# Attention in half units: order of scores, maxima, exponentials and copies in a kernel of three transformer-like blocks

## The chip, the cores and the metric

One core of a Trainium2 chip runs the whole program. The metric is the time on the device in microseconds (us) of one execution; the kernel before is told by the median of three runs and one profiled execution. Engines: PE is TensorE (PEld its weight loads), DVE VectorE, ACT ScalarE, POOL GpSimd, SP SyncE, which issues the weights' transfers. Each runs its own instructions in order; they wait for one another by semaphores.

## The reference

A hybrid layer (a gated linear recurrence, sparse attention, gated linear attention, merged, and a feed-forward part) is followed by two blocks (each: half a feed-forward part, a mixer, half a feed-forward part) on 256 tokens and 256 context tokens of width 1024, all in fp32. Cut to what matters here, three attentions, 64 wide heads:

```python
# hybrid layer, 16 heads in 4 groups: compressed, selected and windowed keys, each its own softmax
p = softmax(q @ k.T + bias)            # over 15 compressed, 256 selected, 256 windowed keys
o = g[0] * o_cmp + g[1] * o_slc + g[2] * o_win
# even block: 8 heads in 2 groups, window of 128 and 256 context keys, a sink logit per head
p = softmax(concatenate([s_loc, s_ctx, s_sink]))
# odd block: 8 heads, neighbourhood of the grid with a bias, and 256 context keys
p = softmax(concatenate([s_loc + bias, s_ctx]))
o = p @ v
```

## The kernel before

Weights pass through a ring of three slots in SBUF; TensorE multiplies them in split form (lines 817 to 819: high and low parts), which is most of the program. Between such stages stand three attentions. Each is a loop over units: a unit is (kind, g, t), 4 heads of group g for the 128 queries of tile t. UNITS lists 8 of kind nsa (units 0 to 7, t alternates 0, 1), 8 of kind ev (8 to 15, t = 0 to 3 for each of two g; for t = 2 and 3 the queries are context tokens and only the 256 context keys are scored), 4 of kind od (16 to 19). An nsa unit with t = 0 scores 128 keys per head and kind of key (small), one with t = 1 256 (large).

PSUM holds one unit's scores in banks 0 to 3 (nsa: and the compressed ones in bank 4), two turned batches in banks 5 and 6, and the output in bank 7. A unit goes through the engines so:

- TensorE, scores(u): per head r the product of queries and keys into PSUM; nsa at line 1059 (compressed keys 1046), ev and od at 1079. A head's bank must be free: free(b) waits for part b of the exponentials of unit u - 1 (for nsa r = 0 waits for part 1 and r = 1 for part 3). Two signals, att_score, go out, one when heads 0 and 1 (nsa: 0 and 2) are there, one at the end.
- VectorE, att_max(u): in two halves, each waits for its att_score: bias or mask added in PSUM (2226, 2244), negated maximum (2227, 2246), in ev two small steps for the sink (2251, 2253); signal att_max each.
- ScalarE, att_exp(u, part), four parts: exponentials from PSUM to one of two SBUF buffers, with row sums (1588, compressed 1593; 1600, and 1598 for the sink). Parts 0 and 2 wait for a half of the maxima.
- VectorE, att_norm(u): after all four parts. For nsa it multiplies the exponentials with gate over sum (2263 to 2279); for ev and od it makes four diagonal matrices from the reciprocals (2282, 2283, 2285). Signal att_p.
- TensorE, att_out(u): waits for att_p, then per batch of 128 keys turns the four heads' exponentials (a transpose at 1105, for ev and od a product with the diagonal matrices at 1110), and, one batch behind, multiplies the turned batch with the values (1135; od 1125).
- ScalarE, att_copy(u, i): a turned batch from PSUM to SBUF (1611).
- VectorE, att_done(u): the unit's output from PSUM (2295).

A unit has 3 (nsa, t = 0), 5 (nsa, t = 1), 4 or 2 (ev, t >= 2) batches. The order on each engine is written out by hand. TensorE: scores(u + 1), att_out(u). VectorE: att_norm(u), both halves of att_max(u + 1), att_done(u). ScalarE: copy 0, copy 1, part 0 of u + 1, copy 2, part 1, copy 3, part 2, copy 4, part 3 (copies that a unit doesn't have left out):

```python
for i in range(5):
    if i < len(batches(u)):
        att_copy(u, PT, i)
    if i >= 1 and u + 1 < u1:
        att_exp(u + 1, Pb, i - 1)
```

Of the kernel before, what the change touches and what calls it, by code (L numbers as in the profile page):

```python
# [335 lines left out]
def build(nc, d, out_x):  # L336
# [5 lines left out]
    with ctx:  # L342
# [73 lines left out]
        CMP_AT = 4 * BANK  # L416

# [339 lines left out]
        def _(pe):  # L757
# [273 lines left out]
            def scores(u):  # L1031
# [7 lines left out]
                if kind == "nsa":  # L1039
# [10 lines left out]
                    for r in range(4):  # L1050
                        half = slice(64 * (r % 2), 64 * (r % 2) + 64)
                        if r < 2:
                            free(1 + 2 * r)
                        if r == 2:
                            compressed(0).then_inc(sig("cmp_even"), 1)
                        for seg in range(2):
                            kk = (B_kk if g % 2 == r % 2 else B_ks)[half, 2 * seg + g // 2, 0:nk]
                            at = place(seg, r) * S
                            last = mm(psum[:, at:at + nk], B_q[half, 2 * g + r // 2, t * P:(t + 1) * P], kk,
                                      start=True, stop=True)  # L1060
                        if r == 2:
                            last.then_inc(sig("att_score"), 1)
# [226 lines left out]
        def _(act):  # L1289
# [284 lines left out]
            def att_exp(u, Pb, part):  # L1574
# [3 lines left out]
                nm, sm = small[:, 0:12], small[:, 16:28]  # L1578
# [16 lines left out]
                else:  # L1595
                    k0 = S if t >= 2 else 0
                    if kind == "ev" and part % 2 == 0:
                        A(small[:, 32 + part:34 + part], small[:, 28 + part:30 + part], ACT.Exp)
# [15 lines left out]
            def attention(u0, u1, Pb, PT):  # L1614
# [3 lines left out]
                for u in range(u0, u1):  # L1618
                    for i in range(5):
                        if i < len(batches(u)):  # L1620
                            att_copy(u, PT, i)
                        if i >= 1 and u + 1 < u1:
                            att_exp(u + 1, Pb, i - 1)
# [92 lines left out]
        def _(dve):  # L1716
# [495 lines left out]
            def att_max(u):  # L2212
# [3 lines left out]
                for a in range(2):  # L2216
# [30 lines left out]
                    if kind == "ev":  # L2247
# [5 lines left out]
                        ins = v.tensor_tensor(out=small[:, 28 + 2 * a:30 + 2 * a], in0=sink, in1=nma, op=ALU.add)  # L2253
                    ins.then_inc(sig("att_max"), 1)

            def att_norm(u, Pb):
                kind, g, t = UNITS[u]
                sm = small[:, 16:28]
# [22 lines left out]
                if kind == "ev":  # L2281
                    link(v.tensor_tensor(out=sm[:, 0:4], in0=sm[:, 0:4], in1=small[:, 32:36], op=ALU.add))
                link(v.reciprocal(small[:, 36:40], sm[:, 0:4]))

# [14 lines left out]
            def attention(u0, u1, Pb, y):  # L2299
                att_max(u0)  # L2300
                for u in range(u0, u1):
                    att_norm(u, Pb)
                    if u + 1 < u1:
                        att_max(u + 1)
# [267 lines left out]
```

## Time and profile before

| | |
|---|---|
| median of 3 runs | 2484.18 us (2484.06 to 2491.02) |
| profiled execution | 2482.93 us, its span 2481.0 us |
| PE busy | 2354.6 us (95% of the span) |
| DVE / ACT / POOL busy | 1565.3 / 873.7 / 378.1 us |
| mean granted clock of TensorE | 0.969 of full speed |
| chain that ended last | PE 83%, DVE 10%, ACT 3% |

The page has the engines' busy times, the span in 40 slices with the granted clock of TensorE (1.0 is 2.4 GHz, 0.5 is 1.2 GHz), the chain of waits that ended last, and the costliest groups of instructions by line of the kernel. A TensorE that is busy for 95% of the span leaves some 126 us without work, a good part of them in the attentions. In the views by order of time a row is a merged run of like instructions: start, duration until the end of the last one, engine, line, what is written and read, shapes, count, and in brackets the idle time before it and what ended it. The ends of matmuls are modelled and overlap the next row's start, so starts are compared with starts.

### The profile page before, as it was taken

Reading aid. Unit: us, or ns where it says so; the run is one execution under the profiler, and the core shown is the slowest. Engines: PE = TensorE matmul, PEld = TensorE weight load, DVE = VectorE, ACT = ScalarE, POOL = GpSimd, SP = SyncE. Lnnn points to the kernel's source line nnn. Section 1 sums busy time; section 2 is a strip of 40 time slices with the busy share of each in tenths; the row PEclk is TensorE's granted clock in tenths of the full one; section 3 lists DMA queues with packets and bytes.
Section 4 is the critical chain, followed back from the end, with each engine's and each line's share of the span. In section 5 each row is a group of like instructions: output and inputs, shape, how many; then the busy total and the mean of one; then the engine's idle time right before and its main releaser. Section 6 shows DMA issues by size and latency. Waiting matters only on the chain.

```text
span 2481.0 us, 33593 instructions
## 1 busy us (share of the span) xinstructions
PE 2354.6 (95%) x14384; PEld 2034.6 (82%) x14384; DVE 1565.3 (63%) x1954; ACT 873.7 (35%) x1241; POOL 378.1 (15%) x345
## 2 busy tenths in 40 slices
PE   7999988797999999999989999999999999888999
PEld 7998875597998888888857888888888888777999
DVE  6584545557876887876764977634855434685554
ACT  6744324534444212123443422212422212444332
POOL 0020000121220313120010221201221201101111
PEclk9999987898999999999999999999999999999999
DMA  5453451063653544542300445322445322511453
GB/s 220 170 187 137 141 191 67 1 224 150 252 198 128 200 173 174 199 153 102 107 35 35 167 175 201 136 94 94 165 177 201 136 94 94 153 69 69 170 200 107
DMA packets 34689, 356.29 MB, mean 144 GB/s; under 512 B 3965, under 2 KB 6172, under 8 KB 8428
## 3 DMA queue, kind: packets, MB, share of 16 engines
q1 hardware_dynamic: 31644, 343.67, 37.4%
q0 software_dynamic: 2896, 10.46, 1.6%
q8 instruction: 114, 1.87, 0.3%
q14 instruction: 35, 0.29, 0.0%
HBM read 351.15 MB, written 1.13 MB: 142 GB/s over the span
## 4 chain that ended last, share of the span: by engine, by line
PE 83%; DVE 10%; ACT 3%; issue 2%; DMA 1%; POOL 1%; SPq 0%; DVEq 0%; ACTq 0%
PE psum L817 25%; PE psum L818 24%; PE psum L819 24%; PE psum L1110 2%; DVE ring_r L1740 2%; DVE arena L2340 1%; DMA ring<-in_w 1%; DVE rr L1750 1%; PE psum L1161 1%; ACT arena L1588 1%; PE psum L1105 1%; PE psum L1079 1%; PE psum L1135 1%; PE psum L1015 1%; ACT arena_r L1325 1%
## 5 line engine op out<-in xcount | busy, mean ns | idle before, releaser
L817 PE MATMUL psum<-arena_r 128*128 128x256 f32 (+1 forms) x3368 | 1131.0, 336 | 33.0 <-DVE zT_r L1780 14.4
L819 PE MATMUL psum<-arena_r,ring_r 128*128 128x256 f32 (+1 forms) x3368 | 1121.4, 333 | 0.0
L818 PE MATMUL psum<-zT_r,arena_r 128*128 128x256 f32 (+1 forms) x2640 | 862.2, 327 | 0.0
L1325 ACT ACTIVATE arena_r<-ring 128x2048 fp32r<-128x2048 f32 (+1 forms) x252 | 473.6, 1881 | 844.1 <-PE psum L819 800.9
L1740 DVE TENSOR_TENSOR ring_r<-ring,arena_r 128x2048 fp32r<-128x2048 f32 (+1 forms) x252 | 595.2, 2363 | 214.3 <-ACT arena_r L1325 213.1
L817 PEld LDWEIGHTS psum<-arena_r 128*128 128x128 f32 x3368 | 638.0, 189 | 110.5 <-issue 16.5
L819 PEld LDWEIGHTS psum<-arena_r,ring_r 128*128 128x128 f32 x3368 | 639.7, 190 | 69.2
L818 PEld LDWEIGHTS psum<-zT_r,arena_r 128*128 128x128 f32 x2640 | 503.5, 191 | 46.0
L818 PE MATMUL psum<-arena_r 128*128 128x256 f32 (+1 forms) x1304 | 424.2, 325 | 0.0
L1892 DVE CUSTOM_DVE_ANT_0 psum<-arena,cb 128x1024 f32<-128x1024 f32 x256 | 363.7, 1479 | 0.0
L818 PEld LDWEIGHTS psum<-arena_r 128*128 128x128 f32 x1304 | 246.6, 189 | 20.3
L711 POOL CAST arena_r<-rt 128x512 fp32r<-128x512 f32 (+1 forms) x55 | 57.2, 1039 | 910.4 <-DVE rt L1953 910.4
L1827 DVE SCALAR_TENSOR_TENSOR xT<-psum,gates_h,xT 128x256 f32<-128x256 f32 x168 | 75.3, 479 | 133.7 <-PE psum L819 133.2
L817 PE MATMUL psum<-xT_r,arena_r 128*128 128x256 f32 x512 | 145.4, 284 | 9.0 <-DVE zT_r L1778 8.3
L819 PE MATMUL psum<-xT_r,ring_r 128*128 128x256 f32 x512 | 143.9, 281 | 0.0
L1953 DVE TENSOR_TENSOR rr<-psum,rr 128x512 f32<-128x512 f32 (+1 forms) x55 | 32.1, 584 | 138.6 <-PE psum L819 138.6
L1953 DVE TENSOR_TENSOR rt<-psum,rt 128x512 f32<-128x512 f32 (+1 forms) x55 | 32.1, 584 | 129.2 <-PE psum L819 125.1
L817 PEld LDWEIGHTS psum<-xT_r,arena_r 128*128 128x128 f32 x512 | 97.0, 189 | 12.7 <-issue 12.6
L1308 ACT ACTIVATE arena<-psum 128x256 f32<-128x256 f32 (+3 forms) x98 | 39.4, 410 | 191.2 <-PE psum L819 134.9
L711 POOL CAST arena_r<-rr 128x512 fp32r<-128x512 f32 (+1 forms) x55 | 55.6, 1010 | 336.0 <-DVE rr L1953 336.0
L819 PEld LDWEIGHTS psum<-xT_r,ring_r 128*128 128x128 f32 x512 | 97.1, 190 | 0.0
L713 POOL TENSOR_TENSOR arena_r<-rr,arena_r 128x512 fp32r<-128x512 f32 (+1 forms) x55 | 85.2, 1549 | 4.4
(286 smaller groups left out, 2148.1 us busy)
## 6 DMA issues: line engine op xcount, KB each, us to landing
ring<-in_wf SPq DMA_DIRECT2D x75, 2048.0 KB, 7.9
ring<-in_w SPq DMA_DIRECT2D x42, 2048.0 KB, 7.9
arena<-in_w SPq DMA_DIRECT2D x72, 1024.0 KB, 9.9
ring<-in_wf SPq DMA_DIRECT2D x10, 1536.0 KB, 6.6
ring<-in_w SPq DMA_DIRECT2D x3, 1024.0 KB, 4.9
arena<-strip_scratch POOLq DMA_DIRECT2D x1, 2048.0 KB, 11.6
arena<-rpb_scratch POOLq DMA_DIRECT2D x16, 128.0 KB, 11.3
xT<-in_x SPq DMA_DIRECT2D x1, 1024.0 KB, 6.0
```

What stands on the lines that cost most here:

```text
L711: pool.tensor_copy(hi[:, i, :], a).then_inc(sig("a_hi"), 1)
L713: pool.tensor_tensor(out=lo[:, i, :], in0=a, in1=hi[:, i, :].bitcast(f32), op=ALU.subtract)\
L817: mm(b[c][:, at], whc, xh[:, k, at], start=(k == ks[0]), stop=False)
L818: mm(b[c][:, at], whc, xl[:, k, at], start=False, stop=False)
L819: last = mm(b[c][:, at], wlc, xh[:, k, at], start=False, stop=(k == ks[-1]))
L1110: last = mm(pt[:, r * P:(r + 1) * P], Pb[:, at:at + P], diag, start=True, stop=True)
L1308: A(dst(j), b[0:rows, 0:nt], func, scale=scale).then_inc(evac["A"], 1)
L1325: A(W_hi[h % NHI][:, 0:n], ring[:, half_slot(h)], ACT.Identity).then_inc(sig("w_hi"), 1)
L1740: v.tensor_tensor(out=ring_r[:, at], in0=ring[:, at], in1=W_hi[h % NHI][:, 0:HALVES[h][2]].bitcast(f32), op=ALU.subtract)\
L1827: return v.scalar_tensor_tensor(out=xT[:, k, at], in0=b[:, at], scalar=gate(k, s), in1=xT[:, k, at], op0=ALU.mult, op1=ALU.add)
L1892: v.tensor_tensor_reduce(out=psum[:, at:at + D], in0=src[:, b * D:(b + 1) * D], in1=cb[:, s * D:(s + 1) * D], scale=1.0, scalar=0.0, op0=A ...
L1953: v.tensor_tensor(out=a, in0=b[:, 0:nt], in1=a, op=ALU.mult).then_inc(evac["V"], 1)
```

## The change

It concerns the three attentions alone. (1) The nsa scores come for heads 0, 2, 1, 3, so that the first half is complete after two heads; the compressed keys of the even heads move along before the last head. (2) VectorE computes the first half of the maxima of unit u + 1 before it normalises unit u, the second half after it. (3) ScalarE computes parts 0 and 1 of the exponentials of u + 1 before the first copy of u, part 2 behind copy 1 (behind copy 0 where there are two), part 3 behind the last copy. (4) For that, row sums and sink terms get a place of their own for even and odd units in the tile `small` (own), and VectorE waits, before it overwrites the diagonal matrices, for the turnings of the unit before.

```diff
+        def own(u, a, b):
+            return small[:, 48 * (u % 2) + a:48 * (u % 2) + b]
...
-                    for r in range(4):
+                    for r in (0, 2, 1, 3):
                         half = slice(64 * (r % 2), 64 * (r % 2) + 64)
                         if r < 2:
                             free(1 + 2 * r)
-                        if r == 2:
+                        if r == 3:
                             compressed(0).then_inc(sig("cmp_even"), 1)
...
-                    for i in range(5):
-                        if i < len(batches(u)):
-                            att_copy(u, PT, i)
-                        if i >= 1 and u + 1 < u1:
-                            att_exp(u + 1, Pb, i - 1)
+                    n = len(batches(u))
+                    if u + 1 < u1:
+                        att_exp(u + 1, Pb, 0)
+                        att_exp(u + 1, Pb, 1)
+                    for i in range(n):
+                        att_copy(u, PT, i)
+                        if i == min(1, n - 2) and u + 1 < u1:
+                            att_exp(u + 1, Pb, 2)
+                    if u + 1 < u1:
+                        att_exp(u + 1, Pb, 3)
...
-            def att_max(u):
+            def att_max(u, halves):
...
-                for a in range(2):
+                for a in halves:
...
                 link(v.reciprocal(small[:, 36:40], sm[:, 0:4]))
+                if u > (EV_U if kind == "ev" else OD_U)[0]:
+                    dve.wait_ge(sig("att_turned"), batches_before(u))
...
             def attention(u0, u1, Pb, y):
-                att_max(u0)
+                att_max(u0, (0, 1))
                 for u in range(u0, u1):
+                    if u + 1 < u1:
+                        att_max(u + 1, (0,))
                     att_norm(u, Pb)
                     if u + 1 < u1:
-                        att_max(u + 1)
+                        att_max(u + 1, (1,))
                     att_done(u, y)
```

How it stands on the engines. First VectorE in the od stage, from the output of unit 16 to the maxima of unit 18; lines 2244 and 2246 are a half of the maxima, 2283 and 2285 the normalising of unit 17, 2295 the output. Before:

```order
L2295 COPY arena<-psum 128x2x128 [waits att_mult]
L2283 RECIPROCAL small<-small 128x4 [waits att_exp]
L2285 TENSOR_TENSOR arena<-cst,small 128x512 [waits dve_step]
L2244 TENSOR_TENSOR psum<-psum,arena 128x2x256 [waits att_score]
L2246 TENSOR_REDUCE small<-psum 128x2 [waits dve_step]
L2244 TENSOR_TENSOR psum<-psum,arena 128x2x256 [waits att_score]
L2246 TENSOR_REDUCE small<-psum 128x2 [waits dve_step]
```

After (the same operations at lines 2305, 2252, 2254, 2291, 2295):

```order
L2305 COPY arena<-psum 128x2x128 [waits att_mult]
L2252 TENSOR_TENSOR psum<-psum,arena 128x2x256 [waits att_score]
L2254 TENSOR_REDUCE small<-psum 128x2 [waits dve_step]
L2291 RECIPROCAL small<-small 128x4 [waits att_exp]
L2295 TENSOR_TENSOR arena<-cst,small 128x512 [waits att_turned,dve_step]
L2252 TENSOR_TENSOR psum<-psum,arena 128x2x256 [waits att_score]
L2254 TENSOR_REDUCE small<-psum 128x2 [waits dve_step]
```

The first pair of the maxima, of unit 18, moved ahead of the normalising of unit 17. Second, ScalarE in the same stage: the exponentials of unit 17 (1600) among the copies of unit 16 (1611). Before:

```order
L1611 ACTIVATE arena<-psum 128x512 [waits att_mult,att_turned] x2
L1600 ACTIVATE arena,small<-psum,small 128x512 [waits att_turned,att_max]
L1611 ACTIVATE arena<-psum 128x512 [waits att_mult,att_turned]
L1600 ACTIVATE arena,small<-psum,small 128x512
L1611 ACTIVATE arena<-psum 128x512 [waits att_mult,att_turned]
L1600 ACTIVATE arena,small<-psum,small 128x512 [waits att_max]
L1600 ACTIVATE arena,small<-psum,small 128x512
```

After (lines 1603 and 1614):

```order
L1603 ACTIVATE arena,small<-psum,small 128x512 [waits att_turned,att_max]
L1603 ACTIVATE arena,small<-psum,small 128x512
L1614 ACTIVATE arena<-psum 128x512 [waits att_mult,att_turned] x2
L1603 ACTIVATE arena,small<-psum,small 128x512 [waits att_max]
L1614 ACTIVATE arena<-psum 128x512 [waits att_mult,att_turned] x2
L1603 ACTIVATE arena,small<-psum,small 128x512
```

Two exponentials left the copies' midst, and the fourth alone stands behind the last copy. Third, TensorE in the nsa stage, the scores of a large unit. Before:

```order
L1059 MATMUL psum<-arena 128x256 x4
L1046 MATMUL psum<-arena 128x15 x2
L1059 MATMUL psum<-arena 128x256 x4
L1046 MATMUL psum<-arena 128x15 x2
```

After (lines 1062, 1049):

```order
L1062 MATMUL psum<-arena 128x256 x6
L1049 MATMUL psum<-arena 128x15 x2
L1062 MATMUL psum<-arena 128x256 x2
L1049 MATMUL psum<-arena 128x15 x2
```

The first half's signal went out with the third head and now goes out with the second. In the ev and od stages TensorE's order is as it was.

## Rows read from the trace of the kernel before

**Rows 1.** Stretches: length, PE, PEld, DVE, ACT, POOL busy, clock, DMA share, GB/s.
```profile
387.77:489.25 101.48, 76.93 (x449) 49.83 (x449) 59.55 (x111) 52.86 (x225) 9.75 (x12) 0.73 0.00 1
1257.08:1326.78 69.70, 60.33 (x352) 36.78 (x352) 38.63 (x88) 34.15 (x104) 11.35 (x12) 0.93 0.01 2
2214.38:2255.90 41.52, 38.38 (x289) 26.92 (x289) 19.51 (x27) 21.70 (x49) 6.85 (x12) 0.89 0.00 1
```

**Rows 2.** TensorE by time in od: scores of 18, turning of 17 and 19.
```profile
2230.28 1.99 PE L1079 MATMUL psum<-arena 64*128 64x512 f32 x8
2232.20 2.05 PE L1110 MATMUL psum<-arena 128*128 128x128 f32 x16
...
2249.20 2.05 PE L1110 MATMUL psum<-arena 128*128 128x128 f32 x16 [1.61 <-DVE arena L2285]
```

**Rows 3.** VectorE by time in od.
```profile
2231.83 0.69 DVE L2244 TENSOR_TENSOR psum<-psum,arena 128x512 f32<-128x512 f32 x1
...
2233.70 0.69 DVE L2244 TENSOR_TENSOR psum<-psum,arena 128x512 f32<-128x512 f32 x1
...
2248.24 0.18 DVE L2283 RECIPROCAL small<-small 128x4 f32<-128x4 f32 x1 [0.17 <-ACT arena L1600]
```

**Rows 4.** TensorE by time in ev: units 9, 11 and 15.
```profile
1276.55 1.54 PE L1079 MATMUL psum<-arena 64*128 64x256 f32 x8
1278.54 2.05 PE L1110 MATMUL psum<-arena 128*128 128x128 f32 x16 [0.44 <-DVE arena L2285]
...
1290.12 2.55 PE L1079 MATMUL psum<-arena 64*128 64x512 f32 x8
1292.69 2.05 PE L1110 MATMUL psum<-arena 128*128 128x128 f32 x16
...
1323.46 2.05 PE L1110 MATMUL psum<-arena 128*128 128x128 f32 x16 [2.49 <-DVE arena L2285]
```

**Rows 5.** VectorE by time in ev: output of 8, normalising of 9, maxima of 10.
```profile
1276.67 0.42 DVE L2295 COPY arena<-psum 128x256 f32<-128x256 f32 x1 [4.11 <-PE psum L1135]
1277.38 0.16 DVE L2282 TENSOR_TENSOR small<-small 128x4 f32<-128x4 f32 x1 [0.29 <-ACT arena L1600]
...
1278.40 0.68 DVE L2246 TENSOR_REDUCE small<-psum 128x2 f32<-128x512 f32 x1
...
1279.39 0.68 DVE L2246 TENSOR_REDUCE small<-psum 128x2 f32<-128x512 f32 x1
```

**Rows 6.** TensorE by time in nsa: scores and turning of units 2, 3; unit 7.
```profile
418.41 1.58 PE L1059 MATMUL psum<-arena 64*128 64x256 f32 x5
...
419.99 1.51 PE L1059 MATMUL psum<-arena 64*128 64x256 f32 x10
...
422.89 1.09 PE L1105 MATMUL psum<-cst,arena 128*128 128x128 f32 x8 [1.04 <-DVE arena L2279]
...
428.19 1.22 PE L1059 MATMUL psum<-arena 64*128 64x128 f32 x4
...
434.39 1.97 PE L1105 MATMUL psum<-cst,arena 128*128 128x128 f32 x8 [0.54 <-DVE arena L2279]
...
481.44 1.97 PE L1105 MATMUL psum<-cst,arena 128*128 128x128 f32 x8 [6.93 <-DVE arena L2279]
```

**Rows 7.** VectorE by time in nsa: bias for unit 3's maxima, its normalising.
```profile
422.75 1.22 DVE L2226 TENSOR_TENSOR psum<-psum,arena 128x1024 f32<-128x1024 f32 x1
...
431.05 0.23 DVE L2263 RECIPROCAL small<-small 128x12 f32<-128x12 f32 x1 [2.32 <-ACT arena L1593]
```

**Rows 8.** ScalarE by time in od: an exponential over 512 columns.
```profile
2230.20 0.69 ACT L1600 ACTIVATE arena<-psum,small 128x512 f32<-128x512 f32 x1
```

**Rows 9.** Busy time by stretch in ev, columns as in rows 1.
```profile
1260.00:1264.00 4.00, 1.67 (x5) 0.59 (x4) 3.86 (x6) 1.54 (x5) 3.81 (x5) 0.91 0.01 2
1264.00:1271.00 7.00, 6.13 (x17) 3.04 (x16) 5.15 (x11) 1.54 (x5) 1.26 (x1) 0.51 0.01 2
1320.00:1324.00 4.00, 1.40 (x10) 0.74 (x9) 1.46 (x4) 2.27 (x11) 0.00 (x0) 1.00 0.00 0
```

More of the change, by code:

```diff
@@ L1577, in att_exp @@
                 Pb = Pb[u % 2]
-                nm, sm = small[:, 0:12], small[:, 16:28]
+                nm, sm = small[:, 0:12], own(u, 16, 28)
                 if part % 2 == 0:
@@ L1597, in att_exp @@
                     if kind == "ev" and part % 2 == 0:
-                        A(small[:, 32 + part:34 + part], small[:, 28 + part:30 + part], ACT.Exp)
+                        A(own(u, 32 + part, 34 + part), own(u, 28 + part, 30 + part), ACT.Exp)
                     r = part
@@ L2252, in att_max @@
                                                     op0=ALU.mult, op1=ALU.min))
-                        ins = v.tensor_tensor(out=small[:, 28 + 2 * a:30 + 2 * a], in0=sink, in1=nma, op=ALU.add)
+                        ins = v.tensor_tensor(out=own(u, 28 + 2 * a, 30 + 2 * a), in0=sink, in1=nma, op=ALU.add)
                     ins.then_inc(sig("att_max"), 1)
@@ L2257, in att_norm @@
                 kind, g, t = UNITS[u]
-                sm = small[:, 16:28]
+                sm = own(u, 16, 28)
                 Pb = Pb[u % 2]
@@ L2281, in att_norm @@
                 if kind == "ev":
-                    link(v.tensor_tensor(out=sm[:, 0:4], in0=sm[:, 0:4], in1=small[:, 32:36], op=ALU.add))
+                    link(v.tensor_tensor(out=sm[:, 0:4], in0=sm[:, 0:4], in1=own(u, 32, 36), op=ALU.add))
                 link(v.reciprocal(small[:, 36:40], sm[:, 0:4]))
+                if u > (EV_U if kind == "ev" else OD_U)[0]:
+                    dve.wait_ge(sig("att_turned"), batches_before(u))
                 v.tensor_tensor(out=E_diag if kind == "ev" else O_diag, in0=b3(C("ident"), 4, P),
```

## The prediction

> **What bounds the kernel now.** I read four views, in this order. The page first: TensorE is busy 95% of the span, so the end is set by TensorE, and by its idle time wherever it has to wait. Then the busy time by stretch, for the three attention stages [rows 1]: together 212.7 us of the 2481.0 us span, with TensorE busy for 175.6 us of them, next to no transfers, and a granted clock of 0.73, 0.93 and 0.89. The rest of the program isn't touched and starts right behind each stage, so a microsecond won or lost there should pass straight to the end. Last the order of time on TensorE and VectorE in each stage, to see what ends TensorE's wait before the turning of a unit. I call the last stage O (units 16 to 19), the middle one E (8 to 15), the first N (0 to 7).
>
> In O, TensorE goes from one instruction to the next without a gap: the next unit's scores start at 2230.28 and this unit's turning at 2232.20 [rows 2]. The normalising that the turning needs ran meanwhile, behind the scores. VectorE took up the next unit's maxima only after it, at 2231.83 [rows 3]. In E, TensorE does wait, 0.44 us, for the diagonal matrix of the normalising [rows 4], which in turn waited for the last exponential [rows 5]. In N the gaps are larger: from the start of the next unit's scores to this unit's turning 4.48 us before a small unit and 6.20 us before a large one, and 6.93 us of idle time before unit 7, where no scores are left [rows 6].
>
> **What the change does to that path.** Nothing is added or removed but four-byte columns of a small tile and a wait on VectorE (for turnings) that can't bind: the exponentials awaited just before it stand on ScalarE behind the copies of the unit before, and those behind its turnings. I cost it at nothing; were it to bind it would cost up to one handover, 0.1 us, ten times. What moves is order.
>
> The key is that TensorE's own order of units is untouched: scores of unit u+1 stand behind all of the output work of unit u-1. VectorE now must do the first half of the maxima of u+1 *before* it normalises u, and TensorE must have u normalised before it turns u. So a new chain runs from the end of u-1's output: half of the scores, handover, half of the maxima, normalising, turning. Before, the normalising only had to wait for exponentials and ran beside the scores. What is queued behind VectorE's new wait is thus exactly what TensorE waits for.
>
> *Stage O.* Scores 1.92 us, so 0.96 us for a half [rows 2]. Handover to VectorE 0.12 us: its copy starts at 1276.67 behind multiplications that gave way at 1276.55 [rows 4, 5]. Half of the maxima: 2231.83 to 2233.70, 1.87 us. Normalising with its handover to TensorE: 2248.24 to 2249.20, 0.96 us [rows 2, 3]. Sum 3.91 us, against 1.92 us before: +2.0 us for each of units 17 and 18. For unit 16, whose neighbour's scores wait for its exponentials anyway, between 0 and 2.0; I take 0.7. Unit 19 has no neighbour; its third exponential now runs before the last copies, but VectorE sat idle for only 0.17 us ahead of that normalising [rows 3], as it first has to empty the output of unit 18: -0.2. O: **+4.5 us**, from 3.8 to 5.8.
>
> *Stage E.* Normalising with handover: 1277.38 to 1278.54, 1.16 us. Half of the maxima where only context keys are scored (t = 2, 3): 1278.40 to 1279.39, 0.99 us [rows 4, 5]; where all 512 keys are, 1.87 us as in O and the two small steps for the sink, about 0.35 us, together 2.2. Before the turning of units 9, 10, 13 and 14 (the next unit has t = 2 or 3): half of the 1.54 us of scores less its tail, about 0.6, and 0.12 + 0.99 + 1.16, is 2.85 us against 1.99 us (1276.55 to 1278.54): +0.85 each, 3.4 in all. Before unit 11 (next is a full one): 0.96 + 0.12 + 2.2 + 1.16 = 4.45 us against 2.57 us (1290.12 to 1292.69): +1.9. Unit 12 in the same way, but its scores went slowly in this execution: +0.3. Unit 11 has two batches only, and ScalarE now has the exponential that waits for the second half of the maxima *between* its two copies, so the second copy and the multiplication behind it come late by some 0.7 us. Unit 8 +0.7. Unit 15 has no neighbour and 2.49 us of idle time before it [rows 4]; one pair of its exponentials (over half the columns of the 0.69 us one in [rows 8]) has left the place behind the copies, -0.9. E: 3.4 + 1.9 + 0.3 + 0.7 + 0.7 - 0.9 = **+6 us**, from 4 to 10.
>
> *Stage N.* The scores come as 0, 2, 1, 3, so that the first half is complete after two heads, and needs only the first half of the exponentials; this was the real stall there. Scores of 256 keys take 0.15 us each (ten in 1.51 us), eight of them 1.2 us [rows 6]; half of the maxima of a large unit is 1.22 us for the bias [rows 7] and, as an estimate, as much for the maximum, which reads the same elements, 2.4 us in all; normalising a large unit with its handover takes from 431.05 to 434.39, 3.34 us [rows 6, 7]. A small unit has half the elements; estimates from these are 1.3 us for the maxima and 2.3 us for the normalising. Small unit with a large one next: 1.2 + 0.12 + 2.4 + 2.3 = 6.0 us against 4.48 us, +1.5, and 0.4 us more because the third exponential, which waits for the second half of the maxima, stands before the third copy: +1.9 for units 2, 4, 6. Large unit with a small one next: 0.6 + 0.12 + 1.3 + 3.34 = 5.4 us against 6.20 us: -0.8 for units 1, 3, 5. Unit 0 +0.7. Unit 7: two parts of its exponentials have left the place behind the last copies; each part is two instructions over half the columns of the one of 0.69 us [rows 8], so no less than that, and I take 0.9 to 1: -2 of the 6.93. N: 5.7 - 2.4 + 0.7 - 2 = **+2 us**, from -4 to +7, since the clock mixes two levels here.
>
> *The clock.* At E's start, with 1.67 us of work in 4 us, TensorE fell from 2.4 to 1.2 GHz and stayed there for about 7 us (0.51) [rows 9]; at E's end 1.40 us of work in 4 us left it at 1.00. So gaps of 2 to 2.5 us sometimes cost the clock. The change makes about nine gaps of 1.8 to 2.7 us in E and O, where past the first scores there were two. A fall takes at most half of 7 us, some of it beside other waits; I take one more fall than before, **+2.5 us**, bounds 0 and 15. The Trainium skill (TensorE: Matmul & The Clock Gate, "HAM oscillation — how this bites in real kernels") says that work in bursts with waits between them can lose the clock again at each wait. The stage N agrees with it, at 0.73; by that rule E and O would go the way of N, which is rival 1.
>
> Sum: 4.5 + 6 + 2 + 2.5 = 15 us. The profiled execution took 2482.93 us (span 2481.0 us and 1.9 us around it) and so would take 2498; it is 1.3 us under the median 2484.18 us of the runs shown, so I forecast **2499 us**.
>
> **Rivals.** *1: E and O lose the clock (slower still).* For it: nine such gaps where N, which has such gaps, stands at 0.73. Against it: E held 1.00 through 2.49 us, and its gaps lie between dense matmuls. Price: going from 0.93 to 0.73 means some 40% more of E's and O's 98.7 us of busy TensorE (60.3 + 38.4) [rows 1] at half speed, up to 20 us, of which about 15 on the path beyond the 2.5 counted: 2514 us.
>
> *2: faster.* If the copies of turned batches, queued on ScalarE between exponentials, are what holds the turning, taking two exponentials of 0.69 us [rows 8] from between them saves up to 1.3 us in each of the 17 units with a neighbour, 22 us, more than the 15 us lost: 2477 us. It decides where a copy starts late because of an exponential. Against it: in O, TensorE runs on without idle time between 2232.20 and the next scores, so the copies don't hold it; only in N could part of it be true.
>
> *3: the steadier N pays for the rest.* N's TensorE is busy for 76.9 us at a mean of 0.73 [rows 1], so about half of it at 1.2 GHz. If the evened-out gaps bring half of this up to 2.4 GHz, 19 us of work take half, of which 8 to 10 us are on the path: 2490 us, hardly more than the bound of no change. For it: N's largest gap, 6.93 us, shrinks. Against it: its other gaps grow or stay.
>
> *4: no change.* It would need the half scores to be ready before the exponentials end, that is, ahead of the output work of the unit before on TensorE. The order there isn't changed: 2484 us.
>
> **How the numbers follow.** Forecast 0.74, rival 1 0.12, rival 2 0.04, rival 3 0.07, rival 4 0.03. A measurement of this kernel tells about 0.3%, 7.5 us, from no change. The terms' lower ends (3.8 + 4 - 4 + 0) with part of rival 3 give 2490 us; the upper (5.8 + 10 + 7, and some of the clock) with part of rival 1 2512 us. Rival 3 straddles 2491.7, and the forecast's low tail reaches it too: faster 0.04, same 0.11, slower 0.85.
>
> **What would show it.** In O, turning of units 17 and 18 starts 3.9 us after the neighbour's scores, TensorE's idle time (some 2 us each) ending with the diagonal matrix, and VectorE's maxima stand before the normalising. In E gaps of about 1.8 us, and 2.6 us before units 11 and 12. In N a shorter wait before unit 7, under 5 us, and longer ones before the small units. All three stages grow: O from 41.5 to about 46, E from 69.7 to 76 or more, N by a few microseconds at most. I am wrong if turnings still start right behind the scores in O, if N shrinks by over 8 us, or if time is lost or won outside the three stages.

## The result, and the profile after

The changed kernel takes 2509.7 us, median of 4 runs (2509.24 to 2511.25), against 2484.12 us of the kernel before (4 runs, 2483.2 to 2491.02): ratio 1.0098, 95% interval 1.0079 to 1.0117. It is slower, by 25.6 us where 15 were forecast, and inside the forecast's range; the interval leaves out 1, so the 1% is clear of the noise. The profiled execution has a span of 2507.9 us, 26.9 more than before's.

The three attention stages in the changed kernel, as stretches from the first score to the first matmul behind the stage (length, PE, PEld, DVE, ACT, POOL busy, clock, DMA share, GB/s); they answer to [rows 1]:

```profile
390.02:497.07 107.05, 79.73 (x448) 50.83 (x449) 56.40 (x111) 54.14 (x225) 6.56 (x12) 0.78 0.00 1
1265.19:1346.36 81.17, 61.63 (x352) 38.35 (x352) 39.22 (x88) 34.56 (x104) 11.01 (x12) 0.87 0.01 2
2233.67:2284.01 50.34, 42.45 (x289) 29.79 (x289) 19.41 (x27) 22.00 (x49) 6.46 (x12) 0.82 0.00 1
```

N grew by 5.6 us, E by 11.5, O by 8.8: 25.9 us. What lies outside them has 1.0 us more. So the stages have the whole loss. The share of a stage at 1.2 GHz follows from the clock column, twice one less the clock, times the length: N 55 us before and 47 now, E 10 and 21, O 9 and 18.

TensorE by time in O: turning of unit 16, scores of 18, turning of 17, scores of 19, turning of 18 (start, length, engine, line, idle time before and what ended it), answering to [rows 2]:

```profile
2244.21 3.78 PE L1113 MATMUL psum<-arena 128*128 128x128 f32 x16 [0.99 <-DVE arena L2295]
...
2252.95 1.99 PE L1082 MATMUL psum<-arena 64*128 64x512 f32 x8
2256.95 2.05 PE L1113 MATMUL psum<-arena 128*128 128x128 f32 x16 [2.01 <-DVE arena L2295]
...
2263.65 1.99 PE L1082 MATMUL psum<-arena 64*128 64x512 f32 x8
2267.65 2.49 PE L1113 MATMUL psum<-arena 128*128 128x128 f32 x16 [2.01 <-DVE arena L2295]
```

VectorE in the same place, answering to [rows 3]:

```profile
2254.13 0.70 DVE L2252 TENSOR_TENSOR psum<-psum,arena 128x512 f32<-128x512 f32 x1 [0.62 <-PE psum L1082]
2254.86 1.23 DVE L2254 TENSOR_REDUCE small<-psum 128x2 f32<-128x1024 f32 x1
2256.01 0.17 DVE L2291 RECIPROCAL small<-small 128x4 f32<-128x4 f32 x1
2256.21 0.69 DVE L2295 TENSOR_TENSOR arena<-cst,small 128x512 f32<-128x512 f32 x1
2256.82 0.69 DVE L2252 TENSOR_TENSOR psum<-psum,arena 128x512 f32<-128x512 f32 x1
```

This is the new chain, link by link: the scores start at 2252.95, half of them have reached VectorE at 2254.13 (1.18 us), the half maxima last until 2256.01 (1.88), and the diagonal matrix releases the turning at 2256.95 (0.94). TensorE stands idle for 2.01 us where it went on without a gap before.

TensorE in E: scores of unit 10 and turning of 9, the second multiplication of 10, scores of 12 and turning of 11, then the turnings of 12, 13 and 14, answering to [rows 4]:

```profile
1284.74 1.13 PE L1082 MATMUL psum<-arena 64*128 64x256 f32 x8
1287.64 2.05 PE L1113 MATMUL psum<-arena 128*128 128x128 f32 x16 [1.76 <-DVE arena L2295]
...
1300.08 0.65 PE L1138 MATMUL psum<-arena 128*64 128x256 f32 x4 [0.25 <-ACT arena L1614]
1300.66 1.99 PE L1082 MATMUL psum<-arena 64*128 64x512 f32 x8
1305.25 2.63 PE L1113 MATMUL psum<-arena 128*128 128x128 f32 x16 [2.60 <-DVE arena L2295]
...
1315.49 2.64 PE L1113 MATMUL psum<-arena 128*128 128x128 f32 x16 [3.55 <-DVE arena L2295]
...
1326.61 3.44 PE L1113 MATMUL psum<-arena 128*128 128x128 f32 x16 [1.76 <-DVE arena L2295]
...
1337.76 2.05 PE L1113 MATMUL psum<-arena 128*128 128x128 f32 x16 [1.76 <-DVE arena L2295]
```

The gaps are 1.76 and 2.60 us, and 3.55 before unit 12. The last two rows are the same work behind the same gap: the first took 3.44 us since the clock fell to 1.2 GHz just behind its start, the second 2.05.

In N, TensorE (answering to [rows 6]) and then VectorE ([rows 7]), scores of unit 5 and normalising of unit 4, and unit 7's turning:

```profile
446.65 2.01 PE L1062 MATMUL psum<-arena 64*128 64x256 f32 x11
...
488.91 1.97 PE L1108 MATMUL psum<-cst,arena 128*128 128x128 f32 x8 [4.41 <-DVE arena L2287]
```

```profile
448.68 1.23 DVE L2234 TENSOR_TENSOR psum<-psum,arena 128x1024 f32<-128x1024 f32 x1 [1.48 <-PE psum L1062]
449.94 1.22 DVE L2235 TENSOR_REDUCE small<-psum 128x4 f32<-128x1024 f32 x1
451.08 0.22 DVE L2271 RECIPROCAL small<-small 128x12 f32<-128x12 f32 x1
```

VectorE gets the half scores 2.03 us after their start, not 1.2 + 0.12 as I had it. Unit 7's wait is 4.41 us instead of 6.93.

The waits before the turnings, as idle time of TensorE itself. In E and O together this is the last number of the row

```profile
L1113 PE MATMUL psum<-arena 128*128 128x128 f32 x320 | 50.0, 314 | 21.3 <-DVE arena L2295 21.3
```

and in N, at line 1108, it is 23.9 us. In the kernel before the same two are 6.7 and 11.5 us, so 27.0 us of idle time were added there, about what the stages grew by, 25.9. (The view of one line by `--source` gives 51.3 and 49.0 us, since it adds the idle time of the weight loads, PEld, to that of PE; it counts each wait about twice.) Two smaller parts go against one another. TensorE's waits for exponentials ahead of N's scores fell from 10.2 to 2.3 us, and in E and O more of the work ran at 1.2 GHz, which the runs on the clock take up below.

### The profile page after: what moved, and what is told of

It is laid out like the page before. It is cut to its first block, busy times and chain, and to the rows that moved or that the text cites. A ratio compares the mean times of both kernels' runs of the same rounds, so it can differ in the third digit from the quotient of the medians.

```text
span 2507.9 us, 33603 instructions
## 1 busy us (share of the span) xinstructions
PE 2364.9 (94%) x14384; PEld 2041.5 (81%) x14384; DVE 1562.8 (62%) x1954; ACT 875.6 (35%) x1241; POOL 374.3 (15%) x345
## 3 DMA queue, kind: packets, MB, share of 16 engines
q8 instruction: 114, 1.87, 0.3%
## 4 chain that ended last, share of the span: by engine, by line
PE 84%; DVE 11%; ACT 2%; issue 2%; DMA 1%; POOL 1%; SPq 0%; DVEq 0%; ACTq 0%
PE psum L820 24%; PE psum L821 24%; PE psum L822 24%; PE psum L1113 2%; DVE ring_r L1748 2%; DVE arena L2352 1%; PE psum L1138 1%; PE psum L1108 1%; DMA ring<-in_w 1%; DVE rr L1758 1%; PE psum L1082 1%; PE psum L1164 1%; DVE arena L2283 1%; PE psum L1018 1%; ACT arena_r L1328 1%
```

## The experiments

All runs are given with the length and granted clock of each stage, read from the same stretches as above. The kernel before ran beside each group: 2485.8, 2484.72, 2484.7 and 2485.57 us. Stage lengths come from one execution each, but a stage that an edit leaves alone repeats within 0.3 us from program to program: E is 69.7 us in before, scores_only and before_fill, and 81.2 and 81.3 in changed and after_fill.

| kernel | us | ratio (95%) | N, clock | E, clock | O, clock |
|---|---|---|---|---|---|
| before | 2484.12 | | 101.5, 0.73 | 69.7, 0.93 | 41.5, 0.89 |
| changed | 2509.70 | 1.0098 (1.0079-1.0117) | 107.1, 0.78 | 81.2, 0.87 | 50.3, 0.82 |
| scores_only | 2484.35 | 0.9995 (0.9986-1.0005) | 101.6, 0.75 | 69.7, 0.93 | 41.3, 0.90 |
| vector_old | 2504.73 | 1.0082 (1.0064-1.0099) | 112.0, 0.65 | 76.3, 0.87 | 45.2, 0.90 |
| scalar_old | 2509.54 | 1.0100 (1.0084-1.0115) | 108.1, 0.76 | 83.5, 0.86 | 50.1, 0.85 |
| filler | 2515.25 | 1.0122 (1.0106-1.0137) | 107.1, 0.78 | 87.5, 0.94 | 52.8, 0.89 |
| filler2 | 2506.08 | 1.0080 (1.0062-1.0097) | 106.9, 0.78 | 79.3, 0.94 | 47.1, 0.91 |
| early | 2491.12 | 1.0022 (1.0013-1.0032) | 108.9, 0.69 | 69.7, 0.93 | 43.9, 0.90 |
| best | 2487.01 | 1.0008 (0.9997-1.0019) | 105.4, 0.71 | 68.9, 0.93 | 41.5, 0.89 |
| before_fill | 2479.63 | 0.9978 (0.9968-0.9987) | 99.6, 0.90 | 69.7, 0.93 | 41.5, 0.89 |
| after_fill | 2503.45 | 1.0068 (1.0050-1.0086) | 103.3, 0.90 | 81.3, 0.87 | 50.3, 0.82 |
| best_fill | 2473.74 | 0.9955 (0.9938-0.9971) | 99.9, 0.90 | 68.9, 0.93 | 41.8, 0.89 |
| best_fill2 | 2475.53 | 0.9965 (0.9951-0.9978) | 95.5, 0.93 | 69.4, 0.93 | 40.8, 0.93 |

**Taking the change apart.** The theory is the chain of half scores and half maxima ahead of the normalising. The rivals are the other two moves: the order of scores in N, and the exponentials ahead of copies.

*scores_only*: the kernel before with the order of heads of the change and nothing else.

```diff
-                    for r in range(4):
+                    for r in (0, 2, 1, 3):
...
-                        if r == 2:
+                        if r == 3:
                             compressed(0).then_inc(sig("cmp_even"), 1)
```

> The kernel before with the order of heads 0, 2, 1, 3 alone. Chain theory (the loss comes from VectorE taking the first half of the maxima ahead of the normalising): nothing changes on that path, the time stays at 2484 us, within 3 us, and the first attention at 101 us within 3. Rival (the order of heads is itself the loss in the first attention, because heads 0 and 2 use the same half of TensorE's rows and no longer run side by side): the scores of a unit take about 1 us longer, but as they run beside the normalising the stage grows by at most 2 us; in the kernel after, where they stand on the path, the same effect would be worth 0.5 to 0.7 us a unit.

No change, in any stage. As long as VectorE takes both halves together, their order is free.

*vector_old*: the changed kernel with VectorE's order of before.

```diff
                 for u in range(u0, u1):
-                    if u + 1 < u1:
-                        att_max(u + 1, (0,))
                     att_norm(u, Pb)
                     if u + 1 < u1:
-                        att_max(u + 1, (1,))
+                        att_max(u + 1, (0, 1))
                     att_done(u, y)
```

> The changed kernel with VectorE's order of before (normalising, then both halves of the maxima); ScalarE's new order and the new order of heads stay. Chain theory: turning starts right behind the scores again (1.9 us after their start in the last attention), but ScalarE's copies now queue behind two exponentials that wait for maxima made only after the normalising, so the output work of a unit grows by about 2 us in its place: total 2502 to 2510 us, no gain. If VectorE's order were the whole cause and ScalarE's order free, the time would go back to 2484 us.

Here are TensorE and ScalarE of that run in O:

```profile
2249.24 1.99 PE L1082 MATMUL psum<-arena 64*128 64x512 f32 x8
2251.16 2.05 PE L1113 MATMUL psum<-arena 128*128 128x128 f32 x16
2254.49 0.66 PE L1128 MATMUL psum<-arena 128*64 128x128 f32 x8 [1.28 <-ACT arena L1614]
```

```profile
2252.51 0.69 ACT L1603 ACTIVATE arena<-psum,small 128x512 f32<-128x512 f32 x1 [3.24 <-DVE small L2254]
2253.09 0.19 ACT L1603 ACTIVATION_READ_ACCUMULATOR arena<-psum,small 128x1 f32 x1
2253.18 0.68 ACT L1603 ACTIVATE arena<-psum,small 128x512 f32<-128x512 f32 x1
2253.75 0.20 ACT L1603 ACTIVATION_READ_ACCUMULATOR arena<-psum,small 128x1 f32 x1
2253.85 1.08 ACT L1614 ACTIVATE arena<-psum 128x512 f32<-128x512 f32 x2
```

The gap ahead of the turning is gone, as the chain theory says. Another has come behind it: the first copy stands behind two exponentials, and these wait for maxima that come after the normalising. Three such waits (0.94, 1.28 and 1.48 us) make up the 3.7 us that O is longer than before, at an unchanged clock. So ScalarE's move alone is a loss too, by another wait. Most of this run's loss lies in N, 10.5 us longer than before at a clock of 0.65; how much of that is the clock wasn't separated.

*scalar_old*: the changed kernel with ScalarE's order of before.

```diff
-                    if u + 1 < u1:
-                        att_exp(u + 1, Pb, 0)
-                        att_exp(u + 1, Pb, 1)
-                    for i in range(n):
-                        att_copy(u, PT, i)
...
+                    for i in range(5):
+                        if i < len(batches(u)):
+                            att_copy(u, PT, i)
+                        if i >= 1 and u + 1 < u1:
+                            att_exp(u + 1, Pb, i - 1)
```

> The changed kernel with ScalarE's order of before (exponentials between the copies); VectorE's new order and the new order of heads stay. Chain theory: the gap before each turning stays (2.0 us in the last attention, 1.8 and 2.6 in the middle one), the first attention grows as its last exponentials are late again: total 2510 to 2518 us. Rival (the exponentials ahead of the copies are the loss): back to 2484 to 2490 us.

All three stages are within 2.4 us of the changed kernel, and the time, 2509.54 us, is just under the 2510 to 2518 expected. The gaps before the turnings of 17 and 18 are 2.01 and 2.02 us, as the chain theory has it. VectorE's move alone therefore brings O's whole loss (50.1) and E's (83.5). The two moves' losses don't add up (3.7 and 8.6 us in O, 8.8 together), because with the half maxima ahead of the normalising the exponentials are released in time to be done before the first copy.

*early*: the half scores themselves are moved, which takes them off the chain. TensorE computes the first half of the scores of unit u+2 inside the output work of unit u; VectorE takes their maxima behind the normalising of u and the second half of u+1's.

```diff
+                    scores(u0 + 1)
+                    for u in range(u0, u1):
+                        nxt = u + 2 < u1
+                        att_out(u, Pb, PT, (lambda: scores(u + 2, (0,))) if nxt else None)
+                        if nxt:
+                            scores(u + 2, (1,))
...
+                att_max(u0 + 1, (0,))
                 for u in range(u0, u1):
-                    if u + 1 < u1:
-                        att_max(u + 1, (0,))
                     att_norm(u, Pb)
                     if u + 1 < u1:
                         att_max(u + 1, (1,))
+                    if u + 2 < u1:
+                        att_max(u + 2, (0,))
                     att_done(u, y)
```

> The changed kernel with the first half of each unit's scores moved on TensorE into the output work of two units before (before its last 3 or 4 operations), and VectorE's first half of the maxima moved accordingly to behind the normalising. Theory (the half scores and half maxima in front of the normalising are what costs): with them ahead of the path the gaps of 1.8 to 2.0 us before the turnings go, E falls from 81.2 to 69 to 72 us, O from 50.3 to 42 to 45, N from 107.1 to about 98 to 103; time 2480 to 2488. Rival (ScalarE's exponentials ahead of the copies cost in any order of the others, as in the run with VectorE's old order, E 76.3 and O 45.2): E stays at 76 or more and O at 45 or more, time 2493 to 2500.

TensorE of that run in O:

```profile
2242.34 1.13 PE L1084 MATMUL psum<-arena 64*128 64x512 f32 x4
2243.40 1.16 PE L1117 MATMUL psum<-arena 128*128 128x128 f32 x8
2244.49 1.42 PE L1132 MATMUL psum<-arena 128*64 128x128 f32 x16
2245.84 1.20 PE L1084 MATMUL psum<-arena 64*128 64x512 f32 x4
2247.46 2.05 PE L1117 MATMUL psum<-arena 128*128 128x128 f32 x16 [0.42 <-DVE arena L2313]
```

E is back at before's 69.7 us and O at 43.9, with ScalarE's new order in place: all of E's 11.5 us and 6.4 of O's 8.8, the clock's share included, belonged to the half scores standing behind the output work. The rival, at least 76 and 45, falls. N missed its 98 to 103 us: it took 108.9, at a clock of 0.69, and so the time, 2491.12 us, lies above the 2480 to 2488 expected, though below the rival's 2493. That led to the runs on the clock in N.

**The clock.** The forecast gave it 2.5 us. Products of constants whose result nobody reads were put where TensorE waits, so that the order of the real work is that of the changed kernel and only the idleness is taken away.

*filler* has four of them, *filler2* two, behind the next unit's scores in E and O. The edit of *filler2*:

```diff
                     if u + 1 < u1:
                         scores(u + 1)
+                        if u0 >= 8:
+                            for i in range(2):
+                                mm(psum[:, 4 * BANK:5 * BANK], C("blk64"), cst[:, 0:BANK], start=True, stop=True)
                     att_out(u, Pb, PT)
```

> The changed kernel with four products of constants (128 by 512, into a bank that nothing reads) behind the scores of each next unit in the middle and last attention, where TensorE has its gap of 1.8 to 2.6 us; they change no output. Clock theory (about 5 us of the loss in the two stages is TensorE at 1.2 GHz after such gaps): the granted clock of both stages past their first scores is 1.00, the middle one shrinks from 81.2 to 75 or 76 us, the last from 50.3 to 47, total 2501 to 2504 us. Rival (the clock costs nothing there, the gaps are all): both stages stay within 1.5 us or grow, 2508 to 2512 us.

> The changed kernel with two products of constants behind the next unit's scores in E and O, instead of the four of the run filler, each 0.92 us long (3.70 us for four at 2.4 GHz there), so 1.85 us, which is the length of the gaps of 1.8 to 2.0 us and delays no turning. Theory of the clock (the gaps let the clock fall, and that is about 5 us of E's growth and 2 to 4 of O's): E 75 to 78 instead of 81.2, O 46.5 to 48.5 instead of 50.3, granted clock 0.93 or more in E, time 2501 to 2504. Rival (gaps have little to do with the falls): E and O as in the changed kernel within 1 us, time 2508 to 2511.

*filler* was a bad instrument: four products took 3.70 us in gaps of 1.8 to 2.0 and delayed each turning by some 1.6 us. Its clock was 1.00 in E and O behind their beginnings, as the theory has it, but both stages grew by the delays, and the time, 2515.25 us, lies above both ranges; it says nothing on the price of the clock. With two products, each turning came as far behind the one before as in the changed kernel or less far: unit 10's 9.56 us behind unit 9's in both, unit 13's 9.56 instead of 11.12 us behind unit 12's. Stretches of *filler2*: E from 1279.2 us on, behind its beginning, then all of E and of O. Under them E from 1279.2 us on in the changed kernel:

```profile
1279.20:1344.47 65.27, 59.15 (x363) 35.68 (x362) 27.30 (x70) 29.97 (x89) 3.70 (x4) 1.00 0.00 1
1265.13:1344.47 79.34, 69.65 (x381) 39.53 (x381) 39.23 (x88) 34.59 (x104) 11.03 (x12) 0.94 0.01 3
2232.94:2280.03 47.09, 44.02 (x301) 28.70 (x301) 19.41 (x27) 22.03 (x49) 6.47 (x12) 0.91 0.00 1
```

```profile
1279.20:1346.36 67.16, 51.19 (x328) 33.52 (x327) 27.34 (x70) 29.90 (x89) 3.69 (x4) 0.92 0.00 1
```

The changed kernel has 0.92 there, that is, some 10 us at 1.2 GHz; filled, it has none. Gaps of 1.02, 1.64 and 1.75 us were left in it. The products cost something themselves: unit 8's turning came 2.9 us later, since part of them ran there at 1.2 GHz, and unit 16's 0.4 us later. And as it came later, unit 8's turning ran at 2.4 GHz, which it doesn't in the kernel before either (2.98 us there, 2.05 at 2.4 GHz): 0.9 us that the change didn't add. The clock's part in what the change added is then, as an estimate, 81.17 - 79.34 + 2.9 - 0.9 = 3.8 us in E and 50.34 - 47.09 + 0.4 = 3.7 us in O, 7.5 us in all. Because of the 2.9, E's 79.3 us lie above the 75 to 78 expected and the time 2 us above its range.

The Trainium skill (TensorE: Matmul & The Clock Gate, "HAM oscillation — how this bites in real kernels") describes a kernel whose clock is lost again at every wait, with waits of some 3 to 5 us. The falls here came behind shorter gaps too, of 1.76, 2.01 and 2.60 us besides one of 3.55, and not behind each gap.

**N.** *before_fill*, *after_fill* and *best_fill* put such products, of 384 columns, into the gaps of N alone. The edit of *after_fill* (n is 1 in N and 0 elsewhere, and four more stand behind the scores of unit 0; *before_fill* has 1 and 7 for 3 and 5, and 2 ahead of the second head of a small unit):

```diff
+            def fill(n):
+                for i in range(n):
+                    mm(psum[:, 5 * BANK:6 * BANK - P], C("blk64"), cst[:, 0:BANK - P], start=True, stop=True)
...
                 for u in range(u0, u1):
                     if u + 1 < u1:
                         scores(u + 1)
+                    fill((3 if u + 1 < u1 else 5) * n)
                     att_out(u, Pb, PT)
```

> The kernel before with products of constants (384 columns, 0.69 us each at 2.4 GHz by the 0.92 us of 512 columns) where TensorE waits in stage N alone: 4 behind the scores of unit 0, 2 ahead of the second head of a small unit, 1 behind the scores of each next unit, 7 ahead of unit 7's turning. Theory (N's 54.6 us at 1.2 GHz are a cost of its gaps, about 10 us on the path): N falls from 101.5 to 90 to 96 us at a clock of 0.9 or more, time 2474 to 2480. Rival (the clock is not held by such fillers, or they delay as much as they win): N 99 to 105, time 2482 to 2488.

> The changed kernel with the same products in stage N alone: 4 behind the scores of unit 0, 3 behind those of each next unit (its gaps there are 3.0 to 3.3 us), 5 ahead of unit 7's turning. Theory (the order alone, with the clock held, costs N about 7 us, more than the 5.6 of the traces, in which N of the changed kernel was longer at 2.4 GHz): N stays 5 to 9 us longer than in the run before_fill, 97 to 103, time 2500 to 2506. Rival (N's growth is the clock's doing): N within 3 us of before_fill's.

N of before_fill, then of after_fill:

```profile
389.90:489.50 99.60, 86.21 (x496) 51.15 (x496) 59.38 (x111) 52.59 (x225) 9.76 (x12) 0.90 0.00 1
```

```profile
391.72:495.03 103.31, 91.52 (x508) 58.17 (x508) 56.41 (x111) 53.40 (x225) 6.56 (x12) 0.90 0.00 1
```

The clock rose to 0.90 in both, but N of before_fill fell by only 1.9 us, not by 6 to 11. The distances between turnings show why. Those that end at the turnings of units 3, 5 and 7 are 11.50, 11.49 and 11.49 us in the kernel before, at clocks of 0.57, 0.73 and 0.75, and the same in before_fill at 0.85, 0.94 and 1.00: there the path runs through the other engines, and TensorE's clock isn't on it. Those that end at units 2 and 4 fell by 1.0 and 1.4 us, and the products held up unit 0's turning by 0.5 and unit 6's by 0.6 us. The medians of the two kernels are 5.1 us apart. The profiled executions are only 2.2 us apart, N's 1.9 us and 0.3 outside the stages, so where the rest lies is not shown.

N of after_fill fell by 3.7 us. At equal clocks the changed order costs N 3.7 us, less than the 5 to 9 I expected and more than the rival's 3. The products differ in number between the two, so what N's order alone costs is settled only to about 4 to 6 us.

**A version that beats both.** *best* has N as in early, except that ScalarE computes the fourth part of the exponentials ahead of the last two copies of a large unit, and E and O with VectorE's old order; ScalarE has its old order in O, and copies and exponentials in turn in E.

```diff
+                    if u0 == 0:
+                        order = [("e", 0), ("e", 1), ("c", 0), ("c", 1), ("e", 2), ("c", 2), ("e", 3), ("c", 3), ("c", 4)]
+                    elif u0 == 8:
+                        order = [(w, i) for i in range(4) for w in "ce"]
+                    else:
+                        order = [("c", 0), ("c", 1), ("e", 0), ("c", 2), ("e", 1), ("c", 3), ("e", 2), ("e", 3)]
```

> Stage N as in the run early; E and O with VectorE's order of before, and ScalarE's in O as before, in E copies and exponentials in turn (copy 0, exp 0, copy 1, exp 1, ...). Theory of the chain: N 98 to 103 instead of 101.5, E 66 to 69 instead of 69.7, O 41.5 as before; time 2474 to 2482, the first to be under the kernel before. Rival (the clock in N mixes two levels and takes what is won; or the early scores hold TensorE at exponentials): N 102 to 106, time 2484 to 2490.

It didn't beat the kernel before: N took 105.4 us at a clock of 0.71, and the time, 2487.01 us, can't be told from it. The rival came out. With products in N's gaps, it did beat it:

```diff
+                    fill(4)
                     scores(u0 + 1)
+                    fill(1)
...
                         if nxt:
+                            fill(1)
                             scores(u + 2, (1,))
+                            fill(2)
+                        if u + 2 == u1:
+                            fill(4)
```

> The run best (N with early half scores, E with copies and exponentials in turn) with such products in N: 4 behind the scores of unit 0, 1 behind those of unit 1, then 1 ahead of and 2 behind the second half of the scores of each next unit, 4 ahead of unit 7's turning. Theory (best's N was 61.4 us at 1.2 GHz, and that hid what the early half scores win): N falls from 105.4 to 89 to 96 us, E stays at 69, time 2470 to 2478. Rival (early half scores win nothing in N even at 2.4 GHz): N over 96, time 2480 to 2486.

2473.74 us, 11 us under the kernel before of the same group. The profiled executions are 5.7 us apart, and only 2.2 of them lie in the stages. N, at 99.9 us, is longer than the 89 to 96 expected, as the rival has it, but the time is within the theory's range, not the rival's. One filler stood where TensorE had no gap; *best_fill2* takes it out (`fill(1 - u % 2)`) and adds `fill(4)` behind the first scores of E and `fill(1)` behind those of O.

> The run best_fill without the product ahead of the second half of a large unit's scores (TensorE had no gap there, so its 0.8 us were added to the path three times), and with 4 products of 384 columns behind the scores of E's first unit (a gap of 3.44 us, behind which 10.2 us went at 1.2 GHz) and 1 behind those of O's first unit (a gap of 1.16 us). Theory: N 97 to 98.5 instead of 99.9, E 65 to 67.5 instead of 68.9, O 41 to 42; time 2467 to 2472. Rival (the clock falls in E's beginning all the same, or products run at 1.2 GHz and hold the scores up): E 68.5 to 71, time 2473 to 2477.

```profile
388.69:484.18 95.49, 87.72 (x496) 53.96 (x496) 60.47 (x111) 53.03 (x225) 9.55 (x12) 0.93 0.00 1
1251.29:1320.70 69.41, 61.20 (x360) 38.61 (x360) 38.95 (x88) 33.52 (x104) 11.37 (x12) 0.93 0.01 3
```

N is now 6 us shorter than before's, and 4 us shorter than in before_fill at nearly the same clock, with as many products: that is what the early half scores win there, together with ScalarE's order. The stages have 7.0 of the 7.3 us between the profiled executions. E's beginning fell to 1.2 GHz all the same (its clock stays 0.93), and the time lies in the rival's 2473 to 2477 us, so the rival held in E. Both kernels, at 2473.74 and 2475.53 us, are faster than the one before by some 0.4%, clear of the noise, and no difference between the two is shown.

## Why the prediction was right, and where it was off

The mechanism and the sign were right: the half maxima moved ahead of the normalising put half of the scores and half of the maxima on TensorE's path. Term by term:

- **O, forecast +4.5.** The chain was forecast as 0.96 + 0.12 + 1.87 + 0.96 = 3.91 us and measured as 4.00; units 17 and 18 lost 2.0 and 2.1 us. With the clock's 3.7 us taken out, O grew by 5.1 us: unit 16 lost 1.3 us, where I took 0.7 between bounds of 0 and 2.0, and unit 19 won 0.3.
- **E, forecast +6.** With the clock's 3.8 us taken out, 7.7 us. The gaps were 1.76 us (1.8 forecast) and 2.60 (2.6), and from turning to turning units 9 and 13 lost 0.8 and 0.9 us (0.85), unit 11 2.2 (1.9). Unit 11's second copy was late as forecast: in *filler2*, where the clock is whole, its output work takes 4.24 us instead of 3.50, of which 0.7 was forecast. Off were unit 8, which lost nothing (0.7 forecast); units 10 and 14, 1.3 us each and not 0.85, since before the change their turnings started 1.6 us behind the scores and not 1.99 as unit 9's did; unit 15, which won 0.6 and not 0.9; and unit 12, 1.1 us and not 0.3. I had put unit 12's 4.47 us from scores to turning down to one slow execution, but *before_fill* has the same 4.47. In the changed kernel it is 5.54. Of these, 0.95 us is one small step of VectorE (line 2261) that took 1.11 us instead of 0.16, in *filler2* too. It ended when an operation of GpSimd did (line 668, until 1314.40 us; the step until 1314.42), as it does in *filler2* (1315.66 and 1315.67); whether that held it was not tested.
- **N, forecast +2, measured +5.6.** The parts that shrink were right: the intervals that end at the turnings of units 1, 3 and 5 are 0.6 to 0.7 us shorter (0.8 forecast), and the one before unit 7 2.0 us (2 forecast). Unit 0 lost nothing (0.7 forecast). Intervals that end at the turning of units 2, 4 and 6 grew by 3.6, 2.4 and 3.1 us instead of 1.9. The step that failed is "eight of them 1.2 us": I took 0.15 us a score from ten that came interleaved from both halves of the array's rows ([rows 6]). The first half in the order 0, 2 has heads of one half of the rows only, and VectorE got it after 2.03 us. That is 0.7 us in each of the three. The rest of it I can't separate from the clock; *after_fill* and *before_fill*, at equal clocks, are 3.7 us apart.
- **The clock, forecast +2.5, measured +7.5 (E and O).** This is the step that was off most. I counted one fall more than before; with gaps of 1.76 to 3.55 us before every turning of E behind its beginning, E had three falls there and O one, besides more time at 1.2 GHz at O's start. Rival 1 named this and overpriced it: E went to 0.87 and O to 0.82, not to N's 0.73. The term stayed within its bounds of 0 to 15. That the time lies in the range is owed to that width, and not to the term itself.
- **Outside the stages:** 1.0 us. The other kernels, whose program outside the stages is the same, range there from 4.5 us less than the kernel before (*early*) to 2.5 more (*filler2*), so this isn't the change's.
- **The range.** Its lower end doesn't follow from the sum given for it: 3.8 + 4 - 4 + 0 is +3.8, or 2487 us, and a part of rival 3 takes that lower, not to 2490.

The sum of what was measured is 5.6 (N) + 7.7 (E) + 5.1 (O) + 7.5 (clock) + 1.0 = 26.9 us, the difference of the spans. Rival 2, copies held up by exponentials, didn't come out: by scalar_old, taking exponentials out from between the copies wins nothing beside VectorE's new order, and by vector_old it costs beside the old one, since they then stand ahead of the first copy. Rival 3 was half true: N's clock rose from 0.73 to 0.78, and its time at 1.2 GHz fell by 8 us, but its larger gaps took more than that. Rival 4 is what *early* builds by moving the scores, and what the change didn't.

## What to carry to other kernels

Before work of the next unit is put ahead of the work that the bounding engine waits for, look where that engine produces its input: if it does so behind the output work of the unit before, the move makes a new serial chain of half its input, half of the moved work and what stood there. In these runs, halving a unit all but stopped losing in E and O only where the producer's half was moved early too, as in *early*, and it won only in N, and there only with the clock held up by products (*best_fill2*). And gaps of 2 us in TensorE's work are to be priced twice: once by their length, and once by the clock, which here added some 7.5 us in E and O to 12.8 us of chain. A higher clock pays only where TensorE is on the path: N's clock went from 0.73 to 0.90 in *before_fill* and three of its eight intervals stayed as they were.

## What the runs showed of the hardware

- **Scores of heads on one half of the rows don't run beside each other.** Eight of 256 columns in the order 0, 2 take 1.99 us, here in the run best, against ten in 1.51 us when the heads of both halves come interleaved [rows 6]:

```profile
446.61 1.99 PE L1062 MATMUL psum<-arena 64*128 64x256 f32 x8
```

  The whole of a unit's scores takes equally long in both orders; only when the half is ready depends on it. *scores_only*, which changes nothing but the order, begins its large units with eleven in 2.01 us. That the rows of the array are the cause is read from the program's operands, and no run was made that changes the rows alone.
- **The clock fell behind some gaps of 1.76 to 3.55 us and not behind others of the same length.** In E it fell behind the gaps of 2.60 and 3.55 us and behind one of five of 1.76, in O behind the second of two of 2.01 (the turnings behind them took 2.63, 2.64, 3.44 and 2.49 us where 2.05 is the rule). With products in the gaps it stayed at 1.00 for 65 us.
- **Work that only fills a gap must end within it at 1.2 GHz too**: two products took 1.84 us in E at 2.4 GHz and 2.9 us at its start, where TensorE had no gap to fill, and all of it was added to the path.
